# The order of the rotary chunk and the third head ahead of the first scores, in a two-part transformer kernel

## What is computed

```python
def hybrid_layer(x, positions, g_mix, w_in, w_gate, b_gate, rel_bias, ...):
    h = rms_norm_2(x, g_mix)
    (a_q, a_k, a_v, b_qlat, b_kvlat, b_krope,
     c_q, c_k, c_v, c_f, d_val, d_gate) = jnp.split(h @ w_in, split_points, axis=-1)
    out_a = chunk_band_attention(heads(a_q, 4), heads(a_k, 4), heads(a_v, 4), rel_bias)
    q = (rms_norm_2(b_qlat, g_q_lat) @ w_uq).reshape(b, s, 4, 64 + 32)
    q = jnp.concatenate([q[..., :64], apply_rope(q[..., 64:], positions)], axis=-1)
    kv = (rms_norm_2(b_kvlat, g_kv_lat) @ w_ukv).reshape(b, s, 4, 64 + 64)
    k_rot = apply_rope(b_krope, positions)
    ...                                   # out_b: attention of q and (kv, k_rot)
    log_f = jax.nn.log_sigmoid(c_f + b_forget)
    ...                                   # out_c: attention with cumulated log_f; out_d: a convolution of 31 taps
    gates = jax.nn.sigmoid(h @ w_gate + b_gate).reshape(b, s, 4, 1024)
    x = x + jnp.sum(gates * proj, axis=2) @ w_o
    hf = rms_norm_2(x, g_ffn)
    return x + jnp.square(jax.nn.relu(hf @ w_up)) @ w_down
```

## Time and profile before

| | us |
|---|---|
| median of 3 runs | 2814.07 |
| the runs | 2813.23, 2814.07, 2816.17 |
| the profiled execution | 2815.08 |
| its span | 2813.3 |
| busy in the span: TensorE matmul | 2785.0 (99%) |
| VectorE / ScalarE / GpSimd | 1246.7 / 1237.8 / 1232.0 (44% each) |
| mean granted clock of TensorE in the span | 0.996 of full speed |

### The profile page before, as it was taken

How to read it: one execution, slowest core, us unless ns; L and a number is a source line. 1 busy time by engine, 2 the same in 40 slices (tenths; PEclk the granted TensorE clock), 3 DMA queues, 4 the chain that set the end, 5 groups by cost and what they waited for, 6 DMA issues and landing times.

```text
span 2813.3 us, 32448 instructions
## 1 busy us (share of the span) xinstructions
PE 2785.0 (99%) x12950; PEld 2265.7 (81%) x12950; DVE 1246.7 (44%) x2089; ACT 1237.8 (44%) x1805; POOL 1232.0 (44%) x549
## 2 busy tenths in 40 slices
PE   9999999999999999999999999999999999999998
PEld 8886888888778888887777888888877778888887
DVE  4666552544765525336666432021256674420112
ACT  4665442444754334334674443143345744342331
POOL 4222444444554444443455444444434564444443
PEclk9999999999999999999999999999999999999999
DMA  4212332333223323332222323333322222333332
GB/s 152 91 64 65 92 103 90 105 98 97 90 82 98 105 90 99 100 97 80 76 68 90 98 91 97 97 97 98 105 88 71 68 90 90 98 98 98 98 97 75
DMA packets 74726, 259.25 MB, mean 92 GB/s; under 512 B 9856, under 2 KB 9856, under 8 KB 74576
## 3 DMA queue, kind: packets, MB, share of 16 engines
q1 hardware_dynamic: 73280, 255.08, 28.8%
q10 hardware_dynamic: 1296, 2.10, 0.2%
HBM read 254.95 MB, written 2.13 MB: 91 GB/s over the span
## 4 chain that ended last, share of the span: by engine, by line
PE 93%; DVE 3%; ACT 2%; POOL 1%; issue 1%; DMA 0%; SPq 0%; DVEq 0%; ACTq 0%; POOLq 0%
PE ps L442 27%; PE ps L443 27%; PE ps L444 27%; PE ps L508 2%; PE ps L538 2%; PE ps L564 1%; PE ps L521 1%; PE ps L566 1%; PE ps L565 1%; PE ps L490 1%; PE ps L491 1%; PE ps L492 1%; PE ps L453 1%; DVE tmp L1845 0%; POOL w_lo L2007 0%
## 5 line engine op out<-in xcount | busy, mean ns | idle before, releaser
L2007 POOL TENSOR_TENSOR w_lo<-raw,w_hi 128x1024 fp32r<-128x1024 f32 x469 | 1132.5, 2416 | 1478.6 <-ACT w_hi L924 1478.5
L442 PE MATMUL ps<-xs,w_hi 128*128 128x512 f32 x2176 | 862.6, 396 | 1.6 <-DVE xs L1408 1.6
L443 PE MATMUL ps<-xs,w_hi 128*128 128x512 f32 x2176 | 847.9, 390 | 0.0
L444 PE MATMUL ps<-xs,w_lo 128*128 128x512 f32 x2176 | 847.8, 390 | 0.0
L924 ACT ACTIVATE w_hi<-raw 128x1024 fp32r<-128x1024 f32 x470 | 495.0, 1054 | 660.3 <-PE ps L444 620.9
L442 PE MATMUL ps<-hid,w_hi 128*128 128x512 f32 x1316 | 515.8, 392 | 5.6 <-POOL w_lo L2007 2.9
L443 PE MATMUL ps<-hid,w_hi 128*128 128x512 f32 x1316 | 512.8, 390 | 0.0
L444 PE MATMUL ps<-hid,w_lo 128*128 128x512 f32 x1316 | 512.8, 390 | 0.0
L442 PEld LDWEIGHTS ps<-xs,w_hi 128*128 128x128 f32 x2176 | 408.9, 188 | 97.2 <-issue 8.1
L443 PEld LDWEIGHTS ps<-xs,w_hi 128*128 128x128 f32 x2176 | 408.9, 188 | 88.9 <-issue 5.3
L444 PEld LDWEIGHTS ps<-xs,w_lo 128*128 128x128 f32 x2176 | 408.8, 188 | 85.7
(11 more groups left out here) (232 smaller groups left out, 2580.4 us busy)
## 6 DMA issues: line engine op xcount, KB each, us to landing
raw<-in_weights SPq DMA_DIRECT2D x470, 512.0 KB, 3.4
btab<-in_rel SPq DMA_DIRECT2D x8, 256.0 KB, 3.9
out<-tmp ACTq DMA_DIRECT2D x8, 256.0 KB, 2.0
hT<-in_x SPq DMA_DIRECT2D x3, 512.0 KB, 7.3
btab<-in_heads SPq DMA_DIRECT2D x6, 256.0 KB, 3.8
tmp<-in_heads SPq DMA_DIRECT2D x6, 256.0 KB, 3.8
common<-in_fixed SPq DMA_DIRECT2D x1, 642.0 KB, 10.7
hT<-in_x SPq DMA_DIRECT2D x2, 256.0 KB, 4.1
```

Source lines behind the costliest of these rows:

```text
L442: pe.matmul(banks[bank][:], wh, rh, start=(k == 0), stop=False)
L443: pe.matmul(banks[bank][:], wh, rl, start=False, stop=False)
L444: last = pe.matmul(banks[bank][:], wl, rh, start=False, stop=(k == len(specs) - 1))
L2007: gp.tensor_tensor(w_lo[:, n % NPAIR, :], raw[:, n % NRAW, :], w_hi[:, n % NPAIR, :].bitcast(F32), ALU.subtract).then_inc(*w_low.tick(n))
```

## The change

In `before2` the rotary chunk and head 2 change places, and with them the two `ahead` steps of ScalarE that ask for their weights. The order of all other steps stays. The list serves both hybrid layers and all engines.

```diff
         before2 = [("latent", 0), ("by_token", 0), ("latent", 1), ("latent", 2), ("c_head", 0), ("latent_norms", 0),
-                   ("ahead", 1), ("latent_parts", 1), ("ahead", "rope"), ("latent_parts", 0), ("ahead", 2),
-                   ("c_head", 1), ("rope", 0), ("c_head", 2)]
+                   ("ahead", 1), ("latent_parts", 1), ("ahead", 2), ("latent_parts", 0), ("ahead", "rope"),
+                   ("c_head", 1), ("c_head", 2), ("rope", 0)]
```

## The result

| | us |
|---|---|
| before, median of 11 runs | 2814.60 (2812.40 to 2816.28) |
| after, median of 11 runs | 2808.25 (2806.36 to 2809.81) |
| ratio after to before | 0.9978, 95% interval 0.9969 to 0.9986 |
| profiled executions, before and after | 2815.08, 2808.25 |
| their spans | 2813.3, 2806.5 |

The change makes the kernel 0.22% faster, 6.35 us by the medians; the forecast was 2808.1. The interval of the ratio reaches from 0.14 to 0.31%, so that the gain is real is clear, and whether it is over the 0.2% named in the prediction is just likelier than not. The two profiled executions differ by 6.83 us, and the rows show where each part of it comes from.

The account below looks back on a forecast made before the run. TensorE, busy 2785.0 of 2813.3 us, was taken as the bound. 2815.08 - 4.88 (stalls) - 1.57 (slow clock) = 2808.63, or 2807.62 off the median 2814.07; the middle, 2808.1, was forecast, range 2806.0 to 2811.6.

Parts of the forecast that it names:

- The stall: First score of each hybrid layer: TensorE's wait for VectorE's scaling of head 2 goes, 2.44 us a layer, 4.88 in both.
- The clock: Layer 0 behind the first score: the spell at 1.2 GHz goes with the stall, 1.57 us, bounds 0 and 2 x 1.57.
- only the stall is won: Rival: the median may hold no slow spell, or it turns up elsewhere, so only 4.88 us is won; 2809.2, chance 0.24.
- a spell in another place: Sign that the forecast is wrong: a spell at 1.2 GHz shows in another place than beside c_head 3 in layer 0.
- What is late next: VectorE's rotary chain and block 0's minima end some 4 us later behind TensorE; slack to block 1's scores 1.3 us, cost nothing.
- the wait moves to the scores of block 1: Rival: block 0's minima come over 1.3 us later than worked out, giving back part of the gain; 2809.2 to 2814, chance 0.07.
- the minima's cost without any cover: Between the scores of blocks 0 and 1: without the 6.39 us of covering matmuls, block 0's minima would cost 5.1 us a layer.
- ScalarE and GpSimd: Weight conversions behind block 0's minima move 1.45 us later, the key copy 0.8 late against TensorE; low half's slack 2.6, cost nothing.
- The slower rival: Rival: GpSimd contention holds nine VectorE operations between the rotary product and block 1, 0.7 us longer each; 2820.7, chance 0.05.
- The sum: Whole kernel: 4.88 and 1.57 us off the profiled execution give 2808.63, off the median 2807.62; the middle, 2808.1, is forecast.
- the bound of 0.2%: Whole kernel: about 5.6 us, the least a measurement can tell from no change, at 2808.4; the forecast stands just beyond it.

Follow-up runs that it names:

- before_again1: The kernel before, unchanged, profiled once more to look for spells at 1.2 GHz; one execution, 2816.24 us.
- t_alone: The changed kernel with VectorE's list put back in the order of before, all other engines in the new order; 2821.08 us, ratio 1.0022.

## Why the prediction was right

**The stall.** 2.44 us a layer was forecast and 2.44 was measured in each. The gap from last matmul to score is 0.32 us in both layers, as taken from another score. That VectorE's queue was the cause was inferred from a row, and is now shown by moving VectorE's step alone.

**The clock.** 1.57 us was forecast for layer 0, 1.61 measured. I called it the less certain term, with bounds of 0 and twice the value. The choice of 1.57 was right for the trace that it was read from; that the kernel before has one such spell at its two stalls, not none or two, in each of three traces, the prediction could not know, and what decides where it falls stays open. In the one trace of each kernel with a single stall, the spell stands behind the stall that is left, so it goes only with both. The rival *only the stall is won* rested on the belief that the median might hold no spell; no trace bears it out. The prediction's last sign of being wrong, a spell in another place, does show in the trace of after, behind the wait at 798 us; but that place is ahead of the change, and before_again1 has it as well.

**What is late next.** The minima of block 0 end 5.60 us behind the first score (forecast 5.5) and the slack to block 1 is 1.17 us (forecast 1.3). The cost is nothing, as said, and the two memsets confirm it. The rival *the wait moves to the scores of block 1* did not happen, but eight memsets make it happen, at the place and in the way described. The prediction put the minima's cost without any cover at 5.1 us a layer. Without c_head 3, but with the key product's three matmuls (0.68 us) left, 4.05 us was measured, so 4.7 by an estimate.

**ScalarE and GpSimd.** ScalarE makes two high halves back to back and the key copy follows at 1284.25; GpSimd's two low halves follow each other:

```profile
1282.23 2.00 ACT L924 ACTIVATE w_hi<-raw 128x1024 fp32r<-128x1024 f32 x2
1284.25 0.59 ACT L974 ACTIVATE att<-ps 64x512 f32<-64x512 f32 x1
```

```profile
1283.35 4.77 POOL L2007 TENSOR_TENSOR w_lo<-raw,w_hi 128x1024 fp32r<-128x1024 f32 x2 [7.11 <-ACT w_hi L924]
```

The copy stands 1.46 us behind block 1's scores. In layer 1 of the kernel before it stood 0.57 behind them (2079.93 in the earlier trace rows):

```profile
2080.50 0.60 ACT L974 ACTIVATE att<-ps 64x512 f32<-64x512 f32 x1
```

It is 0.9 late, forecast 0.8. The first low half is ready at 1285.7 for a reader at about 1288.3.

**The slower rival.** The nine operations kept their lengths (0.70, 0.74, 0.70, 0.69, 0.68, then the tables and minima as in the earlier trace rows), with GpSimd idle beside them as worked out. Contention does show right behind, at 1286.42 in the timeline above: the normalizing operation of block 0 on 128 columns takes 1.78 us, where the like one at 1288.31 takes 0.29. It ends at 1288.20, just when GpSimd's low halves end (1283.35 + 4.77 = 1288.12). The second of them had begun at about 1285.74, ahead of the operation. The Trainium skill (SBUF — State Buffer, Who interferes with whom) states that a VectorE operation in a two-port mode and a GpSimd operation shut each other out for the whole instruction, and that the one issued first goes first; the trace agrees in both, and the prediction had named this operation. That it ran in a two-port mode is not shown. It costs nothing here: its reader, the first transposition, comes later, and TensorE's list has no wait for it in the hybrid layers.

**The sum.** The middle between the two bases, 2808.1, is 0.15 from the median. This was partly luck: medians of the same kernel before came out at 2814.07, 2814.60, 2814.88 and 2814.94. What differed between the profiled executions outside the change was only 0.26 us, and this was luck too, 1.87 us won and 1.6 lost again ahead of the change; the last matmul ahead of the first score starts between 1275.96 and 1277.06 us in the three traces of the kernel before, and at 1275.70 and 1276.86 in the two of the changed one. Nearest to the edge was the bound of 0.2%: 6.2 us by the ratio, against 5.6.

## What to carry to other kernels

Where one list orders several in-order queues, look for the operand whose producer is done on one engine but queued behind something less urgent on the next; moving it gives what the stall shows, as long as a piece of work of known length covers the lateness on either side. Write down that slack in microseconds, as it says how much the next edit may add: here 1.2 us, used up by two memsets. When a stall of TensorE goes, look at the granted clock behind all stalls of its kind, since a spell at 1.2 GHz may only move to the next one as long as one is left, as the trace with layer 0 alone changed showed.

## What the runs showed of the hardware that I had not expected

Equal stalls of 2.4 us are not followed by equal clocks: five of eight had a spell at 1.2 GHz behind them. Which of the two had it was the same in all three traces of the kernel before, but did change when the other stall was taken away (0.65 of full speed from 2070 to 2074 with layer 0's stall gone, 1.00 in that place in all three traces before). At the waits of 2.9 and 2.5 us of the first stack it changed from execution to execution of one kernel, and there a spell behind the first cost nothing by itself: the second wait, for GpSimd, was 0.9 us in its place. Stalls of 3.9 to 4.4 us all had one, half of them twice as long; the longer one in t_alone cost 2.9 us by the starts of its matmuls, against 1.6. And a memset of 0.48 us that waits for the one ahead of it on its own engine takes 0.66 us of the queue, 0.17 of it idle.
